# Seven block products of a float32 SwiGLU feed-forward: combining them on a seeded PSUM bank, and a third weight sum made by an adding transfer

## The chip, the cores and the metric

One core of one Trainium2 chip runs the whole program. The metric is device time in microseconds of one launch: the median of the runs of the kernel before is 1592.42 us (three runs, 1591.45 to 1592.46).

## The reference, cut to what matters

The reference is a small transformer of float32 arithmetic on 256 tokens of width 1024: two layers of (SwiGLU, mixer, SwiGLU), then two layers of (another mixer, SwiGLU). That makes six SwiGLU stages, called f = 0 to 5 below. Each is

```
gate, up = split(rms_norm(x) @ w_in)        # w_in 1024 x 5632, so 2816 columns each
x = x + factor * (silu(gate) * up) @ w_out  # w_out 2816 x 1024
```

Only these six stages are touched by the change.

## The kernel before, in words

**Numbers and engines.** Every float32 product is made from two rounded parts of each operand. A unit of weights is 128 x 2048 numbers (1 MB). It lands in `raw` (3 slots) or in one of the areas `up_k0`, `up_k1`, `w_sum`, `t2` of `work`; ScalarE writes its rounded part into `whi` (`hi`, L1098), VectorE writes the rest, source minus `whi`, into `wlo` (`lo`, L1614), and TensorE makes three matmuls for each pair of chunks (L2254 to L2256 in `product`). `whi` and `wlo` have 3 slots, used in turn: the rounding of unit u waits until TensorE is done with unit u - 3 (`unit_done`). Each engine works its own list strictly in the order in which the functions below write it out.

**A stage.** 42 units in a fixed order. The gate and up columns are cut into 11 blocks of 256: five "plain" blocks (PLAIN_UNITS, two units of 24 matmuls each) and three groups of two blocks, each group made by the seven products of a fast matrix scheme (SUM_UNITS, seven units of 12 matmuls each, `summed`). The four blocks of the product are gate and up for the two halves of tokens t = 0 and 1. The seven products want combinations of weights (`first_sum`, `second_sum`, `third_sum`, and a fourth that GpSimd's queue makes by an adding transfer, `added_block`) and combinations of the operand (`joined_operand`, `form`, with their two rounded parts `form_hi_part` and `form_lo_part`). Then come 11 down units of 24 matmuls (`down`), each behind the transposes of its activation (`turn`) and their two rounded parts (`product_hi` on ScalarE, `product_lo` on VectorE).

**Start of a stage.** Units 0 to 2 are rounded by the stage before. When the reciprocal norm is ready (GpSimd, L801), ScalarE rounds unit 3 and then makes `silu(0, 0)` and `silu(0, 1)` between its parts of the forms; VectorE makes `joined_operand` (L1700), four forms (L1708), the rest of unit 3, the rest of form 0 (L1712), then `product(0, 0)` and `product(0, 1)` (L1685). TensorE meanwhile makes `plain(1, 0, 0)` and `plain(1, 1, 0)`, then turns the first activation (`turn(b_y, act, 0, 2)`, L2375), which waits for both products; then `plain(1, 0, 1)` and `plain(1, 1, 1)`, which want unit 3, then `summed(0, 0)` (unit 4), then `plain(2, 0, 0)`, which waits for `act_ready` 4, that is for `product(1, 0)` and `product(1, 1)`. In stage 0 `begin_first` rounds unit 3 too.

**A group i.** VectorE: `first_sum` (L1629), `second_sum` (L1636), `third_sum` (L1639), six combinations of 128 x 512 from PSUM (`combine_z`, `_u`, `_w`, `_up1`, `_up0`, `_gate1`, L1654 to L1674) and the products. ScalarE: `first_product` copies the first product out of PSUM (L1144). SyncE issues the loads; the load into `up_k0` for a later group waits for the third sum. In group 0 the down unit 10 (`down(0)`) follows units 8 and 9.

**GpSimd** issues the fourth sum's transfers (L826) in order with the norms, `spread_table` and `attention_bias`, where a step waits for a unit of TensorE.

Of the kernel before, what the change touches and what calls it, by code (L numbers as in the profile page):

```python
# [23 lines left out]
ALU = mybir.AluOpType  # L24
# [52 lines left out]
COMBINED = 6  # L77
Z_AT, U_AT, W_AT, UP1_AT, UP0_AT, GATE1_AT = 1, 2, 3, 4, 5, 6
SUMS = 3
T1_AT, T2_AT, T3_AT = 1, 2, 3  # L80
# [96 lines left out]
class Signals:  # L177


    def __init__(self, sem):  # L180
# [19 lines left out]
        self.gate_bias_landed = sem("gate_bias_landed")  # L200
# [37 lines left out]
        self.p1_sb = sem("p1_sb")  # L238
# [111 lines left out]
def build(nc, a, out):  # L350

    with ExitStack() as ctx:
# [64 lines left out]
        pair_act, q_act = area(12288, TT, BANK), xn[:, 1, 0:BANK].rearrange("p (t c) -> p t c", t=TT)  # L417
        p1 = sb("p1", [P, BANK])
        zw, up1 = xn[:, 0, 0:BANK], xn[:, 0, BANK:D]
# [142 lines left out]
        def _(sp):  # L562
# [31 lines left out]
            def ffn(w_in, w_out, l, rnd, f, beside={}):  # L594
# [65 lines left out]
                for i in range(GROUPS):  # L660
                    if i:
                        sp.wait_ge(s.w_sum_ready, SUMS * (GROUPS * f + i - 1) + T3_AT)
                    up_block(i, 0, up_k0)
                    gate_block(i, 0)
                    if i:
                        sp.wait_ge(s.w_lo_ready, unit(0, rnd) + SUM_UNITS[i - 1][5] + 4)
                    up_block(i, 1, up_k1)
                    plain(2 + i, 0)
                    plain(2 + i, 1)
                    gate_block(i, 1)  # L670
# [6 lines left out]
            for l in range(DEPTH):  # L677
# [19 lines left out]
                def gate_bias(t, half):  # L697
                    at = half * D
                    broadcast(gate[:, t, at:at + D], "mix_gate_bias", l * 2 * D + at, D, s.gate_bias_landed)
# [87 lines left out]
        def _(pool):  # L787
# [32 lines left out]
            def added_block(name, l, rnd, i):  # L820

                pool.wait_ge(s.w_lo_ready, unit(0, rnd) + SUM_UNITS[i][3] + 4)
                for k in range(2):
                    src = bass.AP(tensor=a[name].tensor, offset=l * (D * 2 * F) + (4 + 2 * k) * P * 2 * F + (2 + 3 * i) * FB,
                                  ap=[[2 * F, P], [2 * F * P, 2], [1, BANK]])
                    pool.dma_start(t2[:, 2 * k * BANK:2 * (k + 1) * BANK].rearrange("p (k n) -> p k n", k=2), src, accum_op=ALU.add)\  # L826
                        .then_inc(s.w_added, LOADED)

            def attention_bias(l, rnd):
# [15 lines left out]
            for l in range(DEPTH):  # L845
                (r1, _, _, _), (r2, _, _, _) = ffn_stages_a(l)
                norm(3 * l)
                if l == 0:
                    spread_table(0, r1)
                added_block("ffn1_w_in", l, r1, 0)  # L850
                attention_bias(l, r1 + 4)
                pool.wait_ge(s.consts_a_landed, 16)
                pool.wait_ge(s.bias_landed, 2 * BANDS * GRID_H * LOADED * (l + 1))
                for j in range(BANDS):
                    if j == 1:
                        added_block("ffn1_w_in", l, r1, 2)
# [29 lines left out]
                if l + 1 < DEPTH:  # L886
                    spread_table(l + 1, r2)
                for i in range(GROUPS):
                    added_block("ffn2_w_in", l, r2, i)
# [8 lines left out]
            for l in range(DEPTH):  # L898
# [86 lines left out]
                for i in range(GROUPS):  # L985
                    added_block("w_gate_up_2", l, ffn_stage_b(l)[0], i)
# [14 lines left out]
        def _(act_e):  # L1001
# [87 lines left out]
            def ffn(rnd, f, n, o):  # L1089
# [15 lines left out]
                def summed_hi(i, m):  # L1105
                    source, at = {1: (w_sum, T1_AT), 3: (t2, T2_AT), 4: (w_sum, T3_AT), 6: (t2, 0)}[m]
                    if at:
                        act_e.wait_ge(s.w_sum_ready, SUMS * (GROUPS * f + i) + at)
                    else:
# [21 lines left out]
                def pair_silu(i, t):  # L1131

                    if t == 0:
                        act_e.wait_ge(s.unit_done, unit(0, rnd) + SUM_UNITS[i][2] + 4)
# [1765 lines left out]
```

## Time and profile before

| | |
|---|---|
| median of the runs | 1592.42 us |
| profiled execution | 1590.86 us, span 1589.1 us |
| TensorE matmuls busy | 1566.1 us (99%) |
| VectorE busy | 1274.1 us (80%) |
| ScalarE busy | 902.6 us (57%) |
| GpSimd busy | 210.2 us (13%) |
| DMA | 327.29 MB, 206 GB/s mean |
| TensorE clock granted | 0.998 of full speed |

An engine is busy while one of its instructions runs. A matmul's entry lasts longer than the step from one matmul to the next, because they overlap, so the steps between starts are what counts for TensorE. The profiled execution is 1.6 us shorter than the median.

### The profile page before, as it was taken

Reading aid. Unit: us, or ns where it says so; the run is one execution under the profiler, and the core shown is the slowest. Engines: PE = TensorE matmul, PEld = TensorE weight load, DVE = VectorE, ACT = ScalarE, POOL = GpSimd, SP = SyncE. Lnnn points to the kernel's source line nnn. Section 1 sums busy time; section 2 is a strip of 40 time slices with the busy share of each in tenths; the row PEclk is TensorE's granted clock in tenths of the full one; section 3 lists DMA queues with packets and bytes.
Section 4 is the critical chain, followed back from the end, with each engine's and each line's share of the span. In section 5 each row is a group of like instructions: output and inputs, shape, how many; then the busy total and the mean of one; then the engine's idle time right before and its main releaser. Section 6 shows DMA issues by size and latency. Waiting matters only on the chain.

```text
span 1589.1 us, 18786 instructions
## 1 busy us (share of the span) xinstructions
PE 1566.1 (99%) x7346; PEld 1295.9 (82%) x7346; DVE 1274.1 (80%) x1181; ACT 902.6 (57%) x1000; POOL 210.2 (13%) x271
## 2 busy tenths in 40 slices
PE   8999999999999999999999999999999999999998
PEld 6788888887888878888888788888878888887886
DVE  7888856679887988875677888778888876898886
ACT  6555545645555545555565555566655556665554
POOL 1132112011000013211201000131100002110000
PEclk9999999999999999999999999999999999999999
DMA  9887665567766778766556776561877565277672
GB/s 309 260 235 215 232 209 165 185 212 214 246 194 176 240 231 242 215 225 211 156 177 212 248 236 211 163 218 54 265 221 231 197 191 170 99 253 228 191 211 92
DMA packets 182415, 327.29 MB, mean 206 GB/s; under 512 B 13028, under 2 KB 77944, under 8 KB 182328
## 3 DMA queue, kind: packets, MB, share of 16 engines
q1 hardware_dynamic: 169064, 300.66, 56.8%
q0 software_dynamic: 12960, 24.94, 8.7%
q8 instruction: 58, 0.95, 0.3%
q10 hardware_dynamic: 304, 0.50, 0.1%
q14 instruction: 29, 0.24, 0.0%
HBM read 322.88 MB, written 2.88 MB: 205 GB/s over the span
## 4 chain that ended last, share of the span: by engine, by line
PE 90%; DVE 6%; ACT 2%; issue 1%; POOL 1%; POOLq 0%; DVEq 0%; ACTq 0%
PE pg L2254 18%; PE pg L2256 18%; PE pg L2255 18%; PE acc L2254 10%; PE acc L2256 10%; PE acc L2255 10%; DVE wlo L1614 2%; PE pg L2375 2%; PE pg L2267 1%; DVE xn L1708 1%; DVE xn L1700 1%; DVE work L1639 1%; ACT whi L1098 1%; POOL ms L799 1%; ACT work L1015 0%
## 5 line engine op out<-in xcount | busy, mean ns | idle before, releaser
L2254 PE MATMUL pg<-whi,xTh 128*128 128x512 f32 (+1 forms) x1096 | 436.8, 399 | 0.1
L2256 PE MATMUL pg<-whi,xTl 128*128 128x512 f32 (+1 forms) x1096 | 426.7, 389 | 0.0
L2255 PE MATMUL pg<-wlo,xTh 128*128 128x512 f32 (+1 forms) x1096 | 426.2, 389 | 0.0
L1614 DVE TENSOR_TENSOR wlo<-raw,whi 128x2048 fp32r<-128x2048 f32 x143 | 328.8, 2299 | 51.0 <-ACT whi L1098 48.7
L1098 ACT ACTIVATE whi<-raw 128x2048 fp32r<-128x2048 f32 x143 | 274.1, 1917 | 150.1 <-PE pg L2256 81.9
L1512 DVE TENSOR_TENSOR wlo<-raw,whi 128x2048 fp32r<-128x2048 f32 (+1 forms) x87 | 198.6, 2283 | 59.4 <-ACT whi L1008 59.1
L2254 PEld LDWEIGHTS pg<-whi,xTh 128*128 128x128 f32 x1096 | 206.4, 188 | 43.7 <-DVE xTl L1527 1.4
L2256 PEld LDWEIGHTS pg<-whi,xTl 128*128 128x128 f32 x1096 | 206.1, 188 | 42.8
L1614 DVE TENSOR_TENSOR wlo<-work,whi 128x2048 fp32r<-128x2048 f32 x90 | 208.3, 2314 | 39.1 <-ACT whi L1098 39.1
L2255 PEld LDWEIGHTS pg<-wlo,xTh 128*128 128x128 f32 x1096 | 206.5, 188 | 40.3 <-issue 1.0
L2254 PE MATMUL acc<-whi,bTh 128*128 128x512 f32 (+1 forms) x572 | 227.7, 398 | 8.0 <-DVE wlo L1614 8.0
L1098 ACT ACTIVATE whi<-work 128x2048 fp32r<-128x2048 f32 x90 | 172.5, 1916 | 100.1 <-PE acc L2256 75.0
L2256 PE MATMUL acc<-whi,bTl 128*128 128x512 f32 (+1 forms) x572 | 222.8, 390 | 0.0
L2255 PE MATMUL acc<-wlo,bTh 128*128 128x512 f32 (+1 forms) x572 | 222.3, 389 | 0.0
L1008 ACT ACTIVATE whi<-raw 128x2048 fp32r<-128x2048 f32 (+1 forms) x87 | 165.1, 1899 | 61.6 <-PE acc L2256 37.0
L2254 PEld LDWEIGHTS acc<-whi,bTh 128*128 128x128 f32 x572 | 107.5, 188 | 31.5 <-issue 10.5
L2256 PEld LDWEIGHTS acc<-whi,bTl 128*128 128x128 f32 x572 | 107.4, 188 | 23.0
L2255 PEld LDWEIGHTS acc<-wlo,bTh 128*128 128x128 f32 x572 | 107.6, 188 | 20.5
L1154 ACT ACTIVATE bTh<-pg 128x512 fp32r<-128x512 f32 x66 | 39.6, 599 | 76.9 <-PE pg L2375 76.5
L2254 PE MATMUL pg<-whi,bTh 128*128 128x512 f32 (+1 forms) x178 | 69.3, 390 | 0.0
L2256 PE MATMUL pg<-whi,bTl 128*128 128x512 f32 (+1 forms) x178 | 69.1, 388 | 0.0
L2255 PE MATMUL pg<-wlo,bTh 128*128 128x512 f32 (+1 forms) x178 | 69.0, 388 | 0.0
(276 smaller groups left out, 1955.0 us busy)
## 6 DMA issues: line engine op xcount, KB each, us to landing
raw<-in_ffn_w_in SPq DMA_DIRECT2D x124, 512.0 KB, 5.5
raw<-in_ffn_w_out SPq DMA_DIRECT2D x88, 512.0 KB, 4.6
raw<-in_mix_w_in SPq DMA_DIRECT2D x64, 512.0 KB, 4.6
raw<-in_w_gate_up SPq DMA_DIRECT2D x64, 512.0 KB, 5.5
work<-in_ffn_w_in SPq DMA_DIRECT2D x48, 512.0 KB, 5.7
raw<-in_w_down SPq DMA_DIRECT2D x44, 512.0 KB, 4.4
work<-in_ffn_w_in POOLq DMA_DIRECT2D x24, 512.0 KB, 9.5
raw<-in_w_in SPq DMA_DIRECT2D x24, 512.0 KB, 5.3
```

The lines of the kernel that those rows point to most:

```text
L799: pool.tensor_tensor(sums, mean, eps[:, 0:n], ALU.add).then_inc(ms_sem, 1)
L1008: act_e.activation(whi[:, slot, 0:cols], raw[:, slot, 0:cols], ACT.Copy).then_inc(s.w_hi_ready, 1)
L1098: act_e.activation(whi[:, u % SLOTS, :], source, ACT.Copy).then_inc(s.w_hi_ready, 1)
L1154: act_e.activation(bTh[:, part, :], bank[:, :].rearrange("p (c n) -> p c n", c=2), ACT.Copy).then_inc(s.actT_hi, 1)
L1512: v.tensor_tensor(wlo[:, slot, 0:cols], raw[:, slot, 0:cols], f32(whi[:, slot, 0:cols]), ALU.subtract)\
L1614: v.tensor_tensor(wlo[:, u % SLOTS, :], source, f32(whi[:, u % SLOTS, :]), ALU.subtract).then_inc(s.w_lo_ready, 1)
L1639: v.tensor_tensor(w_sum, up_k0, up_k1, ALU.add).then_inc(s.w_sum_ready, 1)
L1700: v.tensor_tensor(xn[:, :, :].rearrange("p t d -> p (t d)"), f32(xTh[:, :, :]).rearrange("p k n -> p (k n)"), f32(xTl[:, :, :]).rearrange( ...
L2254: pe.matmul(dst, xh, wh, start=first and i == 0, stop=False, skip_group_check=onto)
L2255: pe.matmul(dst, xh, wl, start=False, stop=False, skip_group_check=onto)
L2256: mm = pe.matmul(dst, xl, wh, start=False, stop=last and i == len(pairs) - 1, skip_group_check=onto)
L2375: tr = pe.transpose(bank[:, c * T + t * P:c * T + (t + 1) * P], source[:, t, at + c * P:at + (c + 1) * P], ident[:, :])
```

## The change

- The order of the first six products of a group changes: product 2 is accumulated before product 1, and the order of the 42 units with it (SUM_UNITS, DOWN_UNITS).
- ScalarE copies the first product from bank `pg[0][0]` into bank `pg[0][1]` (`seed`); products 3, 4 and 6 are then accumulated on that bank by TensorE, and product 5 on top of product 1 in the other. Two further copies by ScalarE (`second_product`, `hold`) and two subtractions by VectorE (`combine_up1`, `combine_up0`) take the place of one copy and six combinations.
- VectorE's third sum goes; GpSimd's queue adds the second up block into `up_k0` by two adding transfers after the first sum.
- The activation of a group alternates between two areas; the first two turned activations go to `acc[2]` and `acc[3]`.
- The lists at the start of a stage are reordered on ScalarE and VectorE.

```diff
-SUM_UNITS = ((4, 6, 8, 9, 11, 13, 15), (16, 18, 20, 21, 23, 25, 27), (28, 30, 32, 33, 35, 37, 38))
+SUM_UNITS = ((4, 8, 6, 9, 11, 13, 15), (16, 20, 18, 21, 22, 24, 26), (28, 32, 30, 33, 34, 36, 38))
-DOWN_UNITS = (10, 12, 14, 22, 24, 26, 34, 36, 39, 40, 41)
+DOWN_UNITS = (10, 12, 14, 23, 25, 27, 35, 37, 39, 40, 41)
...
# SyncE, group i
-                        sp.wait_ge(s.w_sum_ready, SUMS * (GROUPS * f + i - 1) + T3_AT)
-                    up_block(i, 0, up_k0)
-                    gate_block(i, 0)
-                    if i:
+                        gate_block(i, 0)
+                        sp.wait_ge(s.w_lo_ready, unit(0, rnd) + SUM_UNITS[i - 1][4] + 4)
+                        up_block(i, 0, up_k0)
                         sp.wait_ge(s.w_lo_ready, unit(0, rnd) + SUM_UNITS[i - 1][5] + 4)
+                    else:
+                        if rnd == 0:
+                            sp.wait_ge(raw_landed[0], 64)
+                        up_block(i, 0, up_k0)
+                        gate_block(i, 0)
...
# GpSimd
+            def third_sum(name, l, f, i):
+
+                pool.wait_ge(s.w_sum_ready, SUMS * (GROUPS * f + i) + T1_AT)
+                added_block(name, l, i, 0, up_k0, s.w_third)
...
+                        if (j, row) == (1, 0):
+                            third_sum("ffn1_w_in", l, 2 * l, 1)
                         if (j, row) == (2, 1):
-                            added_block("ffn1_w_in", l, rnd - 4, 1)
+                            fourth_sum("ffn1_w_in", l, rnd - 4, 1)
...
# ScalarE
+                def seed(i):
+
+                    act_e.wait_ge(s.unit_done, unit(0, rnd) + SUM_UNITS[i][0] + 4)
...
+                    act_e.activation(pg[0][1][:, :], pg[0][0][:, :], ACT.Copy).then_inc(s.p_copied, 1)
+
+                def second_product(i):
...
+                    act_e.activation(up1, pg[0][0][:, :], ACT.Copy).then_inc(s.p_copied, 1)
+
+                def hold(i):
+                    act_e.wait_ge(s.unit_done, unit(0, rnd) + SUM_UNITS[i][3] + 4)
+                    act_e.activation(held[:, :], pg[0][1][:, :], ACT.Copy).then_inc(s.p_copied, 1)
...
-                if f > 0:
+                if f == 0:
+                    silu(0, 0)
+                    silu(0, 1)
+                    form_hi_part(0)
+                    form_hi_part(1)
+                    form_hi_part(2)
+                else:
+                    form_hi_part(0)
+                    silu(0, 0)
+                    form_hi_part(1)
+                    form_hi_part(2)
                     loaded_hi(3)
-                form_hi_part(0)
-                silu(0, 0)
-                silu(0, 1)
-                form_hi_part(1)
-                form_hi_part(2)
+                    silu(0, 1)
                 form_hi_part(3)
...
+                        summed_hi(i, 4)
+                        second_product(i)
+                        silu(2 + i, 1)
+                        loaded_hi(DOWN_UNITS[3 * i])
+                        hold(i)
...
# VectorE
+                if start:
+                    product(0, 0)
+                    product(0, 1)
                 joined_operand()
                 form(0)
                 form(1)
+                form_lo_part(0)
+                if not start:
+                    product(0, 0)
                 form(2)
+                form_lo_part(1)
+                form_lo_part(2)
                 form(3)
                 if not start:
                     loaded_lo(3)
-                form_lo_part(0)
-                product(0, 0)
-                product(0, 1)
-                form_lo_part(1)
+                    product(0, 1)
                 first_sum(0)
                 for i in range(GROUPS):
                     qa, qb = PLAIN_UNITS[2 + i]
                     loaded_lo(SUM_UNITS[i][0])
+                    second_sum(i)
                     if i == 0:
                         product_lo(0)
+                    else:
+                        pair_product(i - 1, 0)
                     loaded_lo(qa)
                     if i == 0:
                         product(1, 0)
                         product(1, 1)
...
# TensorE, group i
+                    copied(i, SEED_AT)
+                    summed(i, 2, b_x, x_block(0, 1), onto=True)
                     plain(2 + i, 0, 1).then_inc(s.ffn_t0_done, 1)
                     plain(2 + i, 1, 1).then_inc(s.unit_done, 1)
-                    pe.wait_ge(s.p1_sb, GROUPS * f + i + 1)
-                    summed(i, 2, b_x, x_block(0, 1), onto=True)
+                    pe.wait_ge(s.silu_ready, ACTS * f + 4 + 4 * i + 1)
...
+                    summed(i, 1, b_x, x_form(0))
...
+                    summed(i, 3, b_y, x_form(2), onto=True)
                     if i:
                         turn_first(i - 1, True)
...
+                    else:
+                        down(0)
+                    copied(i, HELD_AT)
...
+                    summed(i, 4, b_y, x_form(1), onto=True)
+                    if i:
+                        down(3 * i, lambda: turn_first(i - 1, False))
```

## Rows read from the trace of the kernel before

**Rows 1.** The page: engines, and the chain that ended last.

```profile
PE 1566.1 (99%) x7346; PEld 1295.9 (82%) x7346; DVE 1274.1 (80%) x1181; ACT 902.6 (57%) x1000; POOL 210.2 (13%) x271
...
PE 90%; DVE 6%; ACT 2%; issue 1%; POOL 1%; POOLq 0%; DVEq 0%; ACTq 0%
```

**Rows 2.** Waits of TensorE: us in total, times, longest us.

```profile
PE acc L2254 <- DVE wlo L1614: 8.0, 6, 1.3
PE pg L2375 <- DVE work L1685: 6.5, 6, 3.5
```

**Rows 3.** Timeline of the start of stage 3: start us, us, instruction, idle before it.

```profile
866.26 0.55 POOL L801 TENSOR_TENSOR rstd<-ms,neghalf 128x1 f32<-128x1 f32 x1
...
866.85 1.92 ACT L1098 ACTIVATE whi<-raw 128x2048 fp32r<-128x2048 f32 x1 [2.60 <-POOL rstd L801]
866.85 2.29 DVE L1700 TENSOR_TENSOR xn<-xTh,xTl 128x2048 f32<-128x2048 f32 x1 [0.71 <-POOL rstd L801]
...
869.18 2.62 DVE L1708 TENSOR_TENSOR xn<-xn 128x512 f32<-128x512 f32 x4
...
869.90 0.63 ACT L1148 ACTIVATE bTh<-xn 128x512 fp32r<-128x512 f32 x1 [1.13 <-DVE xn L1708]
...
870.55 1.28 ACT L1129 ACT_TABLE_LOAD   x1
...
871.85 0.84 ACT L1129 ACTIVATE work<-pg,rstd 128x256 f32<-128x256 f32 x2
...
871.96 0.39 PE L2254 MATMUL pg<-whi,xTh 128*128 128x512 f32 x1
...
874.46 0.39 PE L2256 MATMUL pg<-whi,xTl 128*128 128x512 f32 x1
874.52 0.87 DVE L1685 SCALAR_TENSOR_TENSOR work<-pg,rstd,work 128x256 f32<-128x256 f32 x2
...
875.44 0.66 PE L2375 MATMUL pg<-ident,work 128*128 128x128 f32 x4 [0.60 <-DVE work L1685]
```

**Rows 4.** The same timeline, up to the second pair of products.

```profile
878.11 2.28 DVE L1614 TENSOR_TENSOR wlo<-raw,whi 128x2048 fp32r<-128x2048 f32 x1
...
880.31 0.68 DVE L1692 TENSOR_TENSOR bTl<-pg,bTh 128x512 fp32r<-128x512 f32 x1
...
880.91 2.28 DVE L1614 TENSOR_TENSOR wlo<-raw,whi 128x2048 fp32r<-128x2048 f32 x1
...
883.11 0.87 DVE L1685 SCALAR_TENSOR_TENSOR work<-pg,rstd,work 128x256 f32<-128x256 f32 x2
...
884.03 0.19 PEld L2254 LDWEIGHTS pg<-whi,xTh 128*128 128x128 f32 x1 [0.17 <-DVE work L1685]
```

**Rows 5.** Timeline of stage 2: its first two silu follow the form directly.

```profile
538.67 0.82 ACT L1129 ACTIVATE work<-pg,rstd 128x256 f32<-128x256 f32 x2
```

**Rows 6.** Timeline of the start of stage 0.

```profile
22.54 2.28 DVE L1700 TENSOR_TENSOR xn<-xTh,xTl 128x2048 f32<-128x2048 f32 x1
...
28.92 1.12 PE L2375 MATMUL pg<-ident,work 128*128 128x128 f32 x4 [3.52 <-DVE work L1685]
...
39.13 0.60 ACT L1144 ACTIVATE p<-pg 128x512 f32<-128x512 f32 x1 [0.43 <-PE pg L2256]
```

**Rows 7.** Groups of instructions by line and form: busy us, mean ns, idle before.

```profile
L1098 ACT ACTIVATE whi<-work 128x2048 fp32r<-128x2048 f32 x90 | 172.5, 1916 | 100.1 <-PE acc L2256 75.0 <-PE pg L2256 14.5 <-DVE work L1639 10.7
...
L1639 DVE TENSOR_TENSOR work<-work 128x2048 f32<-128x2048 f32 x18 | 41.1, 2283 | 0.0
...
L1662 DVE TENSOR_TENSOR xn<-xn,pg 128x512 f32<-128x512 f32 x18 | 12.2, 679 | 0.0
...
L1144 ACT ACTIVATE p<-pg 128x512 f32<-128x512 f32 x18 | 10.8, 601 | 3.0 <-PE pg L2256 2.6
```

**Rows 8.** The adding transfers of line 826, and the DMA queues' shares.

```profile
L826 POOL DMA_DIRECT2D work<-in_ffn_w_in x24: 1204/1487/1790, 55.4 to 997.7; - x24
...
DMA to landing us min/median/max: 5.7/9.4/12.1
```

**Rows 9.** The page: DMA queues, packets, MB, share of 16 engines.

```profile
q1 hardware_dynamic: 169064, 300.66, 56.8%
q0 software_dynamic: 12960, 24.94, 8.7%
```

More of the change, by code:

```diff
@@ L1619, in summed_lo @@
                 def summed_lo(i, m):
[L1620 removed]
+                    lo(SUM_UNITS[i][m], {1: w_sum, 3: t2, 4: up_k0, 5: up_k1, 6: t2}[m])
                 def sums_before(i):
@@ L1759, in ffn @@
-                    loaded_lo(DOWN_UNITS[3 * i])
-                    if i:
+                        loaded_lo(DOWN_UNITS[0])
+                        product(2, 1)
+                        summed_lo(0, 4)
+                        loaded_lo(DOWN_UNITS[1])
+                        summed_lo(0, 5)
+                        combine_up1(0)
+                        loaded_lo(DOWN_UNITS[2])
+                        product_lo(2)
+                        first_sum(1)
+                        summed_lo(0, 6)
@@ L1761, in ffn @@
+                        combine_up0(0)
+                    else:
+                        summed_lo(i, 4)
+                        product(2 + i, 1)
+                        loaded_lo(DOWN_UNITS[3 * i])
                         product_lo(3 * i)
-                    product(2 + i, 1)
-                    combine_u(i)
-                    summed_lo(i, 4)
-                    if i:
+                        summed_lo(i, 5)
+                        combine_up1(i)
+                        loaded_lo(DOWN_UNITS[3 * i + 1])
@@ L2378, in turn_first @@
                 def turn_first(i, first):
-                    turn(pg[1][1 - first], pair_act, 0 if first else FB, ACTS if i == GROUPS - 1 else 4 + 4 * (i + 1) + (1 if first else 2))
+                    turn(pg[1][1 - first], pair_acts[i % 2], 0 if first else FB, ACTS if i == GROUPS - 1 else 4 + 4 * (i + 1) + (1 if first else 2))
                 def turn_plain(i):
@@ L2401, in combined, with copied @@
                     pe.wait_ge(s.combined, COMBINED * (GROUPS * f + i) + at)
+                def copied(i, at):
+                    pe.wait_ge(s.p_copied, COPIES * (GROUPS * f + i) + at)
                 def form_ready(m):
@@ L2450, in ffn @@
                 plain(1, 1, 0).then_inc(s.unit_done, 1)
-                turn(b_y, act, 0, 2)
+                turn(acc[2], act, 0, 2)
                 plain(1, 0, 1).then_inc(s.ffn_t0_done, 1)
@@ L2482, in ffn @@
                     if i == 0:
                         form_ready(1)
-                    summed(i, 4, b_y, x_form(1))
-                    down(3 * i + 1, lambda: turn_plain(i))
-                    pe.wait_ge(s.silu_ready, ACTS * f + 4 + 4 * i + 3)
+                    summed(i, 4, b_y, x_form(1), onto=True)
+                    if i:
+                        down(3 * i, lambda: turn_first(i - 1, False))
+                    else:
+                        down(1, lambda: turn_plain(0))
                     if i == 0:
@@ L2488, in ffn @@
                         form_ready(3)
-                    summed(i, 5, b_x, x_form(3))
-                    if i < GROUPS - 1:
-                        down(3 * i + 2)
+                    summed(i, 5, b_x, x_form(3), onto=True)
+                    if i:
+                        down(3 * i + 1, lambda: turn_plain(i))
+                    else:
+                        down(2)
                     combined(i, UP1_AT)
                     summed(i, 6, b_y, x_block(1, 1), onto=True)
-                down(8, lambda: turn_first(GROUPS - 1, True))
+                    if i:
+                        down(3 * i + 2, (lambda: turn_first(i, True)) if i == GROUPS - 1 else None)
```

235 lines of the change are left out of this document (97 added, 138 removed).

## The prediction

> **What bounds the kernel now.** I read the page first, then TensorE's waits, then the timeline where those waits stand. TensorE has a matmul running for 1566.1 of 1589.1 us and makes 90% of the chain that ended last [rows 1]: nothing shortens the kernel unless TensorE idles less, because the change leaves the number of matmuls and transposes as it is. Its waits in the six stages are two kinds [rows 2]: `down(0)` waits for the rest of unit 10, 8.0 us in six waits, because VectorE makes the third sum ahead of it; and the first turn waits for `product(0, 1)`, 6.5 us in six waits, of which stage 0 alone has 3.5 and the others 0.6 each. So some 14.5 us, under 1%, is all that the change can win. VectorE's busy 80% matters only through what TensorE waits for.
>
> **Scales.** TensorE: 11 steps from 871.96 to 874.46 us [rows 3], 0.227 us a matmul, so a summed unit takes 2.72 us and a plain or down unit 5.44. VectorE: a 128x2048 subtraction or sum gives way to the next instruction after 2.20 us and a 128x512 one after 0.60 [rows 4]; if the next needs its result, 2.28 and 0.69. ScalarE: 1.92 for a unit [rows 7], 0.63 for a form, 0.60 for a 128x512 copy.
>
> **Taken off.** VectorE loses 18 third sums of 2.28 us and 18 times four combinations of 0.68, about 90 us [rows 7]. With it `down(0)` no longer waits: counted from the products that open a stage's group 0, unit 10's rest would be done after some 18.5 us, and TensorE wants it at 19.5. Gain 8.0 us, and this is all that TensorE gains from it, since elsewhere it does not wait.
>
> **Stages 1 to 5, up to the first turn.** This is the largest term. ScalarE rounded unit 3 at once (866.85 us) while VectorE joined the operand; now it comes behind form 2, and `product(0, 1)` comes behind unit 3's rest. I follow stage 3 by the rows of before [rows 3]. The join starts at 866.85, form 0 is done at 869.87, ScalarE rounds it by 870.53, the table load (1.28) ends at 871.83, `silu(0, 0)` (0.48) at 872.33. VectorE, standing in order, makes `product(0, 0)` from 872.36 and form 2 from 872.76 to 873.45. ScalarE rounds form 2 until 874.11 and, overlapping by 0.1, unit 3 from 874.00 to 875.92. VectorE has filled the time with two form rests and form 3, and waits: unit 3's rest 875.95 to 878.24, `product(0, 1)` from 878.15 to 878.62. TensorE starts the turn at 878.67 in place of 875.44. It was there at 874.7, so its wait grows from 0.6 to about 4.0 us.
>
> **From there to `plain(2, 0, 0)`.** VectorE's list from 878.55: first sum 2.20, unit 4 2.20, second sum 2.20 (moved ahead), rest of the turned activation 0.60, unit 5 2.20, two products 0.87, end at 888.82. Before, the products ended at 883.98 [rows 4]. TensorE's own work from the turn to that point took until 884.03, less the 0.17 of waiting [rows 3, 4], so 8.4 us: it would be ready at 887.1, up to 1 us later if matmuls are slow after the longer wait, as in stage 0, whose turn took 1.12 us [rows 6] and not 0.66. VectorE is later, so it sets this point: 4.84 us later than before in stages 1, 3, 4 and 5. Stage 2 has no table load [rows 5], so everything behind the silu is 1.2 us earlier: 3.6. The sum is 4 x 4.84 + 3.6 = 23.0 us. After that VectorE gains on TensorE, as the margins at units 6 (3 us), 7 (3.4) and 8 (3.7) show when its list is laid out, so nothing more is lost and nothing is won back.
>
> The Trainium skill (ScalarE: Activation LUTs, What ACT_TABLE_LOAD costs) states 1283 ns for the load and another 1380 ns of draining for each switch of set. The row has the load at 1.28 us and the silu 0.02 us behind it, so no such drain stands there; by the rule the silu would come 1.38 us later in each of four stages, and the total would be 5.5 us more.
>
> **Stage 0.** The two products move ahead of the join, whose start slips from 22.54 [rows 6] to 23.3. The turn then needs 23.4 and TensorE arrives at 25.25: the 3.5 us go. But VectorE's list (join, four forms, three rests, first sum, unit 4) ends at 35.1, where TensorE wants unit 4 at 31.2; with second sum, activation, unit 5 and two products it reaches 40.9. Before, this point was 38.9 (the copy at 39.13 less 0.2 of latency) [rows 6]. Cost 2.0. The bounds are 0 (the list is as late as before) and 5 (the load of `up_k0`, now held behind unit 3's, lands later).
>
> **The new wait of groups 1 and 2.** Product 4 goes on the bank that `hold` must have copied; between them TensorE has only a turn. Clock zero where unit 19 is done: TensorE finishes 20 at 2.72, 21 at 5.44, and the turn takes about 0.4 (its entry of 0.66 [rows 3] less the overlap with the next matmul, an estimate), so it arrives at 5.8. ScalarE: unit 20's copy from 2.92, a silu, then unit 23 (1.92, overlapped) from 3.86 to 5.78, then `hold` 5.70 to 6.30 by the 0.60 of the copy of before [rows 7]. Wait 0.5 us, twelve times: 6.0 us. A lower bound is zero, if the turn covers it; the upper is 0.9, if ScalarE is late by another small step. In group 0 `down(0)` stands between and covers 5.44 us.
>
> **At nothing.** `seed` (0.6) has a plain unit of 5.44 us beside it; `second_product` is waited for a unit later. Group 0's two copies lie beside the down units. SyncE's loads of `up_k0` wait for a rest that is done some 20 us before the next first sum. The third sum's transfer: two issues on GpSimd at 1.49 us and 9.4 until landed (12.1 at most) [rows 8], so 12 to 15 us after the first sum. Its reader, product 4's unit, is rounded over 20 us after it in group 0. In the first SwiGLU of a layer GpSimd's queue delays group 1's to unit 15 done plus two bias issues; unit 22 can be rounded 16.3 us after unit 15, plus a summed unit: a margin of 3 to 5 us. The bytes are 18.9 MB more, about 6.6% of the DMA engines' time at that queue's present price [rows 9] (8.7% for 24.94 MB), beside 65% in use: room enough.
>
> **Sum.** 23.0 + 2.0 + 6.0 - 8.0 = +23.0 us on the profiled execution's 1590.9, so 1613.9. The median stands 1.6 above that execution: 1615 us.
>
> **Rivals.**
> - *The start costs less* (1596 to 1606): if VectorE or ScalarE finish their lists some 1.5 us sooner in every stage than I laid out, and `hold` is covered, the terms are 5 x 2.5 + 2 - 8, or about +6 to +10. The table load row speaks against it. Chance 0.11.
> - *Faster* (1580): the start's dependencies don't reach the turn, so that the turn's wait stays at 0.6, stage 0's 3.5 goes and `hold` is covered: 1592.4 - 8.0 - 4.5 = 1580. The place is `product(0, 1)` in stages 1 to 5, and the point is 8 us: TensorE arrives 7.9 us after both other engines start, and the chain I count is 11.8 us. It has to be 3.8 us shorter. For it speaks that VectorE has 90 us less to do and that TensorE may hide lateness of weights inside matmul durations. Against it: the matmuls step at 0.227 us nearly everywhere. Chance 0.13.
> - *No change* (1590 to 1595): the start costs about 10 us and is paid by the waits removed. Chance 0.04.
> - *The third sum lands late* (1630 to 1650): the adding transfer is 12 us or slower beside more traffic, the rounding of unit 22 or 34 waits on ScalarE with everything queued behind it, some 2 us in 12 groups on top of the sum. The margin of 3 us decides. Chance 0.06.
> - That the change doesn't do what it says can be left out: the third sum's instruction is gone from VectorE's list.
>
> **How the numbers follow.** The forecast (1606 to 1624) has 0.66. With the lesser cost and a little of the late transfer the range 1597 to 1630 holds 0.8. A difference under 0.2% (3.2 us) can't be told from none here. Faster: 0.13. Same: 0.04. Slower: 0.66 + 0.11 + 0.06 = 0.83.
>
> **What would show it.** In TensorE's waits the line of `down(0)` is gone; the line of the turn has five waits near 4 us (3 in stage 2) and none in stage 0; a new line of matmuls behind the second pair of products; and twelve short waits for ScalarE's copy of the bank. In the timeline unit 3 is rounded behind form 2. If the turn's waits are under 1 us the forecast falls at its main step; if ScalarE waits for the adding transfer, the fourth rival holds.

## The result and the profile after

The changed kernel takes 1622.86 us (median of 4 runs, 1620.67 to 1626.88) against 1591.93 us of the kernel before on the same chip (4 runs, 1589.67 to 1592.46): a ratio of 1.020, 95% interval 1.0176 to 1.0224, so 31 us slower. Forecast were 1615 us and slower, with a range of 1597 to 1630. The profiled execution of the changed kernel took 1624.3 us, with a span of 1622.4.

The page of the changed kernel: busy time of each engine, the two large DMA queues, and the engines on the chain that ended last.

```profile
PE 1580.2 (97%) x7346; PEld 1303.5 (80%) x7346; DVE 1194.0 (74%) x1091; ACT 919.9 (57%) x1036; POOL 249.9 (15%) x307
...
q1 hardware_dynamic: 169064, 300.66, 55.1%
q0 software_dynamic: 22752, 43.82, 15.4%
...
PE 80%; DVE 6%; DMA 5%; ACT 4%; issue 2%; POOL 1%; SPq 0%; POOLq 0%; DVEq 0%; ACTq 0%
```

VectorE has 80 us less to do than before [rows 1] and the kernel is 31 us slower. TensorE runs as many matmuls; its busy time grew by 14 us. Its share of the chain fell from 90% to 80%, and VectorE, ScalarE and DMA transfers took it. GpSimd's queue took 8.7% of the DMA engines' time before [rows 9] and takes 15.4% now.

What TensorE waits for in the changed kernel (engine, tile and line of the waiting instruction, what released it, total us, times, longest us):

```profile
PE acc L2391 <- DVE work L1703: 18.3, 5, 3.9
PE pg L2270 <- DVE wlo L1660: 9.4, 8, 3.8
PE pg L2270 <- ACT held L1178: 2.7, 11, 0.3
PE pg L2270 <- DVE work L1703: 2.5, 2, 1.3
```

The first line is the first turn (`turn_first`), 6.5 us in six waits before [rows 2]; the line of `down(0)` of before, 8.0 us, is gone; the third is the wait for `hold`, and the fourth one for products, in two places. The second, 9.4 us for rests of weight units, is in the forecast only in part (3.78 us of it is unit 4 in stage 0), and what stands behind the rest shows in the same view for ScalarE:

```profile
ACT whi L1118 <- DMA raw<-in_ffn_w_in: 44.4, 16, 7.0
```

The timeline of stage 3, on ScalarE and VectorE from the join to the turn (start, duration, engine, line, operation, out<-in, and in brackets the idle time before it and its releaser):

```profile
883.47 2.29 DVE L1718 TENSOR_TENSOR xn<-xTh,xTl 128x2048 f32<-128x2048 f32 x1 [0.71 <-POOL rstd L807]
...
887.23 1.28 ACT L1151 ACT_TABLE_LOAD   x1
...
888.53 0.47 ACT L1151 ACTIVATE work<-pg,rstd 128x256 f32<-128x256 f32 x1
...
890.69 1.89 ACT L1118 ACTIVATE whi<-raw 128x2048 fp32r<-128x2048 f32 x1
...
892.62 2.29 DVE L1660 TENSOR_TENSOR wlo<-raw,whi 128x2048 fp32r<-128x2048 f32 x1 [0.51 <-ACT whi L1118]
894.83 0.48 DVE L1703 SCALAR_TENSOR_TENSOR work<-pg,rstd,work 128x256 f32<-128x256 f32 x1
...
895.36 0.98 PE L2391 MATMUL acc<-ident,work 128*128 128x128 f32 x4 [3.90 <-DVE work L1703]
```

The join of this stage starts at 883.47, that is 16.62 us later than before [rows 3]. With that offset taken off, unit 3's rest starts at 876.00 (forecast 875.95), `product(0, 1)` at 878.21 (878.15), and the turn at 878.74 (878.67) after a wait of 3.90 us (4.0).

The same stage, ten microseconds on (SPq is SyncE's queue):

```profile
897.80 2.46 POOL L830 DMA_DIRECT2D work<-in_ffn_w_in  x2 [14.37 <-DVE work L1675]
899.73 1.58 SPq L604 DMA_DIRECT2D raw<-in_ffn_w_in  x2
...
910.38 1.92 ACT L1118 ACTIVATE whi<-raw 128x2048 fp32r<-128x2048 f32 x1 [3.94 <-DMA raw<-in_ffn_w_in]
```

The first row is the third sum's two adding transfers, right behind the first sum. The second is the load of unit 7, and ScalarE gets it 10.65 us after the issue. In the kernel before it is the seventh unit loaded and its buffer comes free with unit 3's rest; now unit 6 is loaded ahead of it, so it is the eighth and waits for unit 4's rest.

### The profile page after: what moved, and what is told of

Read it like the earlier page. It is cut to its first block, busy times and chain, and to the rows that moved or that the text cites. A ratio compares the mean times of both kernels' runs of the same rounds, so it can differ in the third digit from the quotient of the medians.

```text
span 1622.4 us, 18719 instructions
## 1 busy us (share of the span) xinstructions
PE 1580.2 (97%) x7346; PEld 1303.5 (80%) x7346; DVE 1194.0 (74%) x1091; ACT 919.9 (57%) x1036; POOL 249.9 (15%) x307
## 3 DMA queue, kind: packets, MB, share of 16 engines
q1 hardware_dynamic: 169064, 300.66, 55.1%
q0 software_dynamic: 22752, 43.82, 15.4%
## 4 chain that ended last, share of the span: by engine, by line
PE 80%; DVE 6%; DMA 5%; ACT 4%; issue 2%; POOL 1%; SPq 0%; POOLq 0%; DVEq 0%; ACTq 0%
PE pg L2270 16%; PE pg L2272 16%; PE pg L2271 16%; PE acc L2270 9%; PE acc L2272 9%; PE acc L2271 9%; DMA raw<-in_ffn_w_in 4%; DVE wlo L1660 2%; ACT whi L1118 2%; PE pg L2283 1%; PE pg L2391 1%; DVE xn L1718 1%; DMA raw<-in_w_gate_up 1%; POOL ms L805 1%; DVE work L1675 1%
## 5 line engine op out<-in xcount | busy, mean ns | idle before, releaser
L2270 PE MATMUL pg<-whi,xTh 128*128 128x512 f32 (+1 forms) x1096 | 441.9, 403 | 11.5 <-DVE wlo L1660 9.0
L2272 PE MATMUL pg<-whi,xTl 128*128 128x512 f32 (+1 forms) x1096 | 430.2, 392 | 0.0
L2270 PEld LDWEIGHTS pg<-whi,xTh 128*128 128x128 f32 x1096 | 208.7, 190 | 59.7 <-DVE wlo L1660 12.5
L2272 PEld LDWEIGHTS pg<-whi,xTl 128*128 128x128 f32 x1096 | 208.4, 190 | 43.6
L2270 PE MATMUL acc<-whi,bTh 128*128 128x512 f32 (+1 forms) x572 | 227.2, 397 | 0.1
L2272 PE MATMUL acc<-whi,bTl 128*128 128x512 f32 (+1 forms) x572 | 223.0, 390 | 0.0
L2272 PEld LDWEIGHTS acc<-whi,bTl 128*128 128x128 f32 x572 | 107.4, 188 | 22.9
L2270 PEld LDWEIGHTS acc<-whi,bTh 128*128 128x128 f32 x572 | 107.5, 188 | 21.1 <-DVE bTl L1710 0.5
L830 POOL DMA_DIRECT2D work<-in_ffn_w_in x48 | 59.3, 1476 | 262.6 <-DVE work L1675 139.4
L2270 PE MATMUL pg<-whi,bTh 128*128 128x512 f32 (+1 forms) x178 | 70.8, 398 | 3.2 <-ACT held L1178 2.7
L805 POOL TENSOR_TENSOR ms<-ss,eps 128x1 f32<-128x1 f32 x16 | 19.2, 1198 | 350.3 <-ACT work L1035 350.3
```

Of the source, the lines that this page charges most:

```text
L805: pool.tensor_tensor(sums, mean, eps[:, 0:n], ALU.add).then_inc(ms_sem, 1)
L830: pool.dma_start(dst[:, 2 * k * BANK:2 * (k + 1) * BANK].rearrange("p (k n) -> p k n", k=2), src, accum_op=ALU.add)\
L2270: pe.matmul(dst, xh, wh, start=first and i == 0, stop=False, skip_group_check=onto)
L2272: mm = pe.matmul(dst, xl, wh, start=False, stop=last and i == len(pairs) - 1, skip_group_check=onto)
```

## The experiments

Two theories stood against each other. *The start*: the order of the two lists at a stage's start makes the turn and `plain(2, 0, 0)` late, as forecast, and the loss falls with it. *The transfers*: the 36 adding transfers delay loads, and the loss falls with them. All kernels ran beside the kernel before, whose median stayed between 1590.99 and 1591.5 us.

### e1_start_order: another order at the start

Of the changed kernel; ScalarE rounds unit 3 while VectorE joins, as before, and both silus come right behind form 0. VectorE's calls move from between the forms, where their lines go, to behind unit 3's rest:

```diff
@@ ScalarE, f > 0
+                    loaded_hi(3)
                     form_hi_part(0)
                     silu(0, 0)
+                    silu(0, 1)
                     form_hi_part(1)
                     form_hi_part(2)
-                    loaded_hi(3)
-                    silu(0, 1)
@@ VectorE, f > 0
                     loaded_lo(3)
+                    form_lo_part(0)
+                    product(0, 0)
                     product(0, 1)
+                    form_lo_part(1)
+                    form_lo_part(2)
                 first_sum(0)
```

> The changed kernel with the lists of ScalarE and VectorE at the start of stages 1 to 5 in the order of the kernel before (unit 3 rounded first, both products behind form 0); the second sum stays where the change put it. Queue-order theory: the five waits at the first turn (18.3 us in the changed kernel) fall to about 0.6 each, but VectorE's list up to plain(2, 0, 0) is only 2.0 us shorter (0.8 in stage 2), because the moved second sum and form 2's rest are still in it, so a new wait of 2 to 3 us appears there and the total falls by only some 9 us, to about 1614. Transfer theory (the extra adding transfers are the main cost): the turn's waits go but the total falls by less than 5 us. If the turn's waits alone were the loss: 16 us or more less, under 1607.

Measured: 1614.64 us, ratio 1.0146 (1.0129 to 1.0163), so 8 us off, as expected. TensorE's waits:

```profile
PE pg L2274 <- DVE work L1703: 13.0, 6, 2.5
...
PE acc L2395 <- DVE work L1703: 3.0, 5, 0.6
```

The turn is back at 0.6 us a stage, as before [rows 2], so the order on record made that wait. VectorE is still late, with 2.5 us at `plain(2, 0, 0)`, since the second sum stands ahead of it.

### e2_second_sum and e3_both: the second sum behind the second pair of products

e2 is the changed kernel with this edit, e3 has e1's too:

```diff
                     loaded_lo(SUM_UNITS[i][0])
-                    second_sum(i)
+                    if i:
+                        second_sum(i)
                     if i == 0:
@@
                         product(1, 1)
+                        second_sum(0)
                         form_lo_part(3)
```

> The changed kernel with only the second sum of group 0 moved back behind the second pair of products. Queue-order theory: the waits at the turn stay at 3.9 us, TensorE is behind anyway, and only the waits of 1.2 to 1.3 us at plain(2, 0, 0) in stages 0 and 2 go: some 3 us less, about 1620. If the second sum were a loss by itself, 5 x 2.2 = 11 us less.

> Both edits together. Queue-order theory: VectorE's list is 4.2 us shorter in each of stages 1 to 5 than in the changed kernel, so about 20 us less, near 1603: more than the sum of the two alone (9 and 3). Transfer theory: 1612 or more.

Measured: e2 1627.6 us (1.023, 1.0215 to 1.0245), e3 1623.82 us (1.0207, 1.0192 to 1.0222). Both are misses, and e3 is the larger: almost no lateness of the start is left in it (the turn's waits are 3.0 us in five), and yet it takes as long as the changed kernel. TensorE's waits in e3:

```profile
PE pg L2276 <- DVE wlo L1660: 24.8, 10, 5.5
```

and the timeline of its stage 1:

```profile
373.73 2.50 POOL L830 DMA_DIRECT2D work<-in_ffn_w_in  x2 [12.44 <-DVE work L1675]
375.50 1.51 SPq L604 DMA_DIRECT2D raw<-in_ffn_w_in  x2
...
389.21 1.91 ACT L1118 ACTIVATE whi<-raw 128x2048 fp32r<-128x2048 f32 x1 [9.83 <-DMA raw<-in_ffn_w_in]
...
393.50 0.80 PE L2276 MATMUL pg<-whi,xTh 128*128 128x512 f32 x1 [5.47 <-DVE wlo L1660]
```

Unit 7's load is issued 1.8 us behind the adding transfers, at 375.50, and ScalarE has it at 389.21, after 13.7 us; TensorE waits 5.47 us at unit 7. What e1 gains at the turn, e3 loses a little further on.

That e2 is slower than the changed kernel is not shown: its runs (1625.12 to 1629.79) overlap with those of the changed kernel (1620.67 to 1626.88), and the spans of the two profiled executions, 1623.2 and 1622.4, differ by 0.8 us. That it isn't 3 us faster its stage 3 explains:

```profile
883.98 2.29 DVE L1718 TENSOR_TENSOR xn<-xTh,xTl 128x2048 f32<-128x2048 f32 x1 [0.71 <-POOL rstd L807]
...
904.14 0.48 DVE L1703 SCALAR_TENSOR_TENSOR work<-pg,rstd,work 128x256 f32<-128x256 f32 x1 [0.73 <-ACT work L1151]
...
906.15 0.39 PE L2272 MATMUL pg<-whi,xTh 128*128 128x512 f32 x1
```

The products of the second pair are done at 904.62, and TensorE comes to `plain(2, 0, 0)` at 906.15, without a wait and 22.17 us behind the join. In the changed kernel that matmul stands at 905.65, 22.18 us behind its join at 883.47. VectorE is early now, and TensorE comes no earlier. In stage 2, where the changed kernel waited 1.34 us for the products, e2 has slow matmuls in place of the wait (shown in the last section).

### e4_third_on_vector and e5_both_vector: the third sum made by VectorE again

e4 is the changed kernel without the 36 adding transfers of `third_sum`, e5 is e3 without them; the sum is made in place:

```diff
             def third_sum(name, l, f, i):
+                return
...
+                def own_third_sum(i):
+                    v.tensor_tensor(up_k0, up_k0, up_k1, ALU.add).then_inc(s.w_third, 2 * LOADED)
...
                     summed_lo(i, 1)
+                    if i:
+                        own_third_sum(i)
                     summed_lo(i, 3)
@@ group 0
                         loaded_lo(DOWN_UNITS[0])
+                        own_third_sum(0)
                         product(2, 1)
```

> The changed kernel with the third sum made by VectorE (in place, up_k0 + up_k1, behind unit 10's rest in group 0 and behind product 2's unit in the others), and the 36 adding transfers of it left out. Transfer theory: ScalarE's waits for raw<-in_ffn_w_in (44.4 us in 16 waits) shrink to some 10 us, the waits of TensorE for wlo (9.4 us in 8) fall by half or more, and the total by 5 to 10 us. Queue-order theory alone: the total stays within 3 us of the changed kernel, because the turn's waits stay and VectorE has room for the sum.

> e3_both with the third sum made by VectorE and its adding transfers left out. New theory after e3_both: with the lists repaired TensorE is earlier, and the next late thing is unit 7's load (issued behind unit 4's rest, 13.7 us to land in stage 1), late because the two adding transfers of the third sum are issued just ahead of it into DMA engines that are 90% busy there. Then TensorE's waits for wlo (24.8 us in 10) fall to some 5 (stage 0's 3.7 stays), and the total to about 1597. Rival (unit 7's load is late because the new order of the units makes it wait for unit 4's rest in place of unit 3's): the waits stay above 15 us and the total above 1610.

Measured: e4 1623.47 us (1.0202, 1.0186 to 1.0217), the time of the changed kernel; e5 1600.03 us (1.005, 1.0033 to 1.0067). The same edit is worth nothing in the one and 24 us in the other. In e4 that is a balance: TensorE waits for unit 7 in no stage, which the changed kernel pays with some 8 us, but VectorE's own sum costs about as much elsewhere. TensorE waits for `hold` 17 times in place of 11 and once 2.1 us for a weight rest, some 5 us together, and behind the turn of stage 5 there are more slow matmuls, 1.3 us. In e3 the waits for unit 7 are far longer, so more is gained. ScalarE's waits for loads of this weight, in e4 and in e5:

```profile
ACT whi L1118 <- DMA raw<-in_ffn_w_in: 17.0, 9, 5.1
...
ACT whi L1118 <- DMA raw<-in_ffn_w_in: 21.2, 11, 5.0
```

Against 44.4 us in the changed kernel and 53.7 in e3: the transfers were what delayed the loads. The order of the units is the new one in e4 and e5 too, so unit 7's later buffer alone costs TensorE nothing there.

### e6_both_deferred: the same bytes, later

e3 again, with the adding transfers of group 0 held until ScalarE has rounded unit 7, so that its load has landed. This tells the amount of traffic from its place:

```diff
                 pool.wait_ge(s.w_sum_ready, SUMS * (GROUPS * f + i) + T1_AT)
+                if i == 0:
+                    pool.wait_ge(s.w_hi_ready, unit(0, FFN_STARTS[f]) + PLAIN_UNITS[2][1] + 1)
                 added_block(name, l, i, 0, up_k0, s.w_third)
```

> e3_both with the adding transfers kept, but those of group 0 held on GpSimd until unit 7's rounded part is made. Theory of the transfers' place: the same bytes at another time, so unit 7 lands in time as in e5_both_vector and the total is about 1598. Rival (adding transfers cost by their amount wherever they are): waits for other units take the place of unit 7's, total above 1610. Rival of the list order: unchanged at 1624.

Measured: 1595.64 us (1.0028, 1.0016 to 1.004; 6 runs), 28 us less than e3 with every byte still moved. Its stage 1, against that of e3 above:

```profile
368.15 0.92 SPq L604 DMA_DIRECT2D raw<-in_ffn_w_in  x2
...
373.59 1.92 ACT L1120 ACTIVATE whi<-raw 128x2048 fp32r<-128x2048 f32 x1 [1.53 <-DMA raw<-in_ffn_w_in]
...
376.22 2.50 POOL L830 DMA_DIRECT2D work<-in_ffn_w_in  x2 [22.28 <-ACT whi L1120]
```

The same load lands in 5.4 us, not 13.7. So it is the place of the transfers and not their amount. e6 is also 4 us faster than e5, which has none of these transfers but VectorE's sum in their stead.

### e7_before_third_late and e9_before_third_early: what `down(0)` costs in the kernel before

Nothing of the change is in these two; only group 0's third sum has another place in VectorE's list. It costs TensorE 8.0 us where it stands [rows 2]. e7, then e9:

```diff
                         summed_lo(i, 3)
-                        third_sum(i)
                         product(2 + i, 0)
@@
                         product_lo(3 * i)
+                    else:
+                        third_sum(0)
```

```diff
                     if i == 0:
-                        summed_lo(i, 3)
                         third_sum(i)
+                        summed_lo(i, 3)
                         product(2 + i, 0)
```

> The kernel before with VectorE's third sum of group 0 moved behind the rest of unit 10, nothing else. If the third sum's place alone made down(0) wait, its 8.0 us go and the ratio is 0.995 (1583); ScalarE's rounding of unit 11 comes 2.3 us later and has down(0)'s 5.4 us to hide in. Rival: the wait moves to unit 11 and the ratio is 1.000.

> The kernel before with VectorE's third sum of group 0 ahead of the rest of unit 9, in the 2.81 us in which VectorE waits there for ScalarE, and nothing else. e7_before_third_late won 4 us and left 4.0 us in six waits for combine_w. If the idle gap takes the sum whole, neither wait is left: 8 us less than the kernel before, ratio 0.995. Rival (the sum pushes unit 9's rest and the wait comes back at unit 9): ratio 0.998 or more.

Measured: e7 1587.37 us (0.9976, 0.9967 to 0.9986; 9 runs), half of what was expected, since the later place brings a new wait at the combination behind it:

```profile
PE pg L2255 <- DVE xn L1662: 4.0, 6, 0.7
```

e9 1581.77 us (0.9939, 0.9927 to 0.9952), 10 us off. VectorE stood idle for 2.81 us behind the first combination of group 0 in stage 3 of the kernel before, waiting for ScalarE. The kernel before:

```profile
898.00 2.29 DVE L1614 TENSOR_TENSOR wlo<-work,whi 128x2048 fp32r<-128x2048 f32 x1 [2.81 <-ACT whi L1098]
```

There the sum now goes (e9):

```profile
891.15 2.28 DVE L1639 TENSOR_TENSOR work<-work 128x2048 f32<-128x2048 f32 x1
894.09 2.29 DVE L1614 TENSOR_TENSOR wlo<-work,whi 128x2048 fp32r<-128x2048 f32 x1 [0.65 <-ACT whi L1098]
```

The idle 2.81 us have become 0.65, and the waits at `down(0)` are gone.

### e8_deferred_hold: `hold` ahead of the down unit

e6, with `hold` moved ahead of the rounding of the down unit, to take away TensorE's short wait for it:

```diff
                         silu(2 + i, 1)
-                        loaded_hi(DOWN_UNITS[3 * i])
                         hold(i)
+                        loaded_hi(DOWN_UNITS[3 * i])
                         product_hi(3 * i)
```

> e6_both_deferred with hold ahead of the rounding of the next down unit on ScalarE in groups 1 and 2. The waits of TensorE for that copy (2.8 us in 11) go to zero: 3 us less than e6_both_deferred. If the wait is the copy's own latency behind product 3, at most 1 us less.

Measured: 1619.77 us (1.0176, 1.0161 to 1.0191), 24 us more than e6 where 3 less were expected. ScalarE now waits at `hold` 21.5 us in twelve waits, and TensorE for the activation's rest:

```profile
PE acc L2278 <- DVE bTl L1712: 20.5, 12, 1.7
```

ScalarE stands in front of `hold` until TensorE is done with the bank, and the rounding behind it comes late by as much, twelve times.

TensorE's wait for `hold` stays as it was, 2.8 us in eleven, so the second of the two cases expected holds: it is the copy's own time and not the rounding ahead of it. The same place in stage 0 of the changed kernel and of e8, the turn, the copy and the matmul that wants it:

```profile
111.31 0.60 PE L2391 MATMUL pg<-ident,work 128*128 128x128 f32 x4
111.50 0.60 ACT L1178 ACTIVATE held<-pg 128x512 f32<-128x512 f32 x1
...
112.15 0.50 PE L2270 MATMUL pg<-whi,bTh 128*128 128x512 f32 x1 [0.25 <-ACT held L1178]
```

```profile
107.35 0.60 PE L2399 MATMUL pg<-ident,work 128*128 128x128 f32 x4
107.55 0.60 ACT L1180 ACTIVATE held<-pg 128x512 f32<-128x512 f32 x1 [1.85 <-PE pg L2280]
...
108.20 0.50 PE L2278 MATMUL pg<-whi,bTh 128*128 128x512 f32 x1 [0.25 <-ACT held L1180]
```

In both, the matmul starts 0.84 to 0.85 us behind the turn. Behind the 111 turns of the changed kernel with no wait it is 0.35 in the median, so each wait costs 0.5 us and the twelve 6.0.

### e10_before_third_start and e11_deferred_start: the start once more

e10 is e9 (the kernel before, third sum moved) and e11 is e6 (the change), both with the products right behind unit 3's rest, and `form_lo_part` 1 to 3 later, behind unit 7's rest in e10 and behind unit 6's in e11. e10's edit:

```diff
@@ ScalarE (stage 0: both silus ahead of form 0)
-                form_hi_part(0)
+                    form_hi_part(0)
                 silu(0, 0)
                 silu(0, 1)
+                if f == 0:
+                    form_hi_part(0)
@@ VectorE
+                if start:
+                    product(0, 0)
+                    product(0, 1)
                 joined_operand()
...
                 form(1)
-                form(2)
-                form(3)
                 if not start:
                     loaded_lo(3)
+                    product(0, 0)
+                    product(0, 1)
+                form(2)
+                form(3)
                 form_lo_part(0)
-                product(0, 0)
-                product(0, 1)
-                form_lo_part(1)
                 first_sum(0)
...
                     if i == 0:
+                        form_lo_part(1)
                         form_lo_part(2)
```

> e9_before_third_early, and at the start of a stage only what the turn needs ahead of it: both products directly behind unit 3's rest (in stage 0 ahead of the joined operand), the rests of forms 1 to 3 behind unit 7's. The turn's waits (0.6 in five stages, 3.5 in stage 0) go; VectorE's list up to plain(2, 0, 0) is 0.6 us shorter, in stage 0 about 3: some 6 us less than e9_before_third_early, ratio 0.991. Rival (VectorE's list, not its order, sets plain(2, 0, 0)): 2 us less or nothing.

> e6_both_deferred with the same start (products behind unit 3's rest, rests of forms 1 to 3 behind unit 6's). The five waits of 0.6 at the turn and of 0.3 at plain(2, 0, 0) go: 5 us less than e6_both_deferred, about 1591, so the change's combining and its adding transfers together come out level with the kernel before. If it were 8 us less, the relief of VectorE would be worth something by itself.

Measured: e10 1577.44 us (0.9911, 0.9896 to 0.9927), the fastest kernel of the study, faster than both kernels and 4.3 us below e9, where 6 were expected; e11 1589.99 us (0.9989, 0.998 to 0.9998; 10 runs). e10's page and TensorE's longest wait in the six stages:

```profile
PE 1564.7 (99%) x7346; PEld 1296.1 (82%) x7346; DVE 1274.2 (81%) x1181; ACT 903.6 (57%) x1000; POOL 210.5 (13%) x271
```

```profile
PE pg L2259 <- DVE wlo L1616: 2.0, 1, 2.0
```

VectorE has its full 1274 us of work and TensorE is 99% busy. The same start on the change (e11) brings it 1.5 us below the kernel before, less than the 3.2 us that can be told from none, and leaves it 12.5 us behind e10.

## Why the prediction was right, and where it was not

**Taken off: right.** The waits of `down(0)` are gone, and that is worth 9.4 us, not 8.0 (see the sum). VectorE's busy time fell by 80 us and not 90, since its entries overlap: by the steps of 2.20 and 0.60 us the 18 sums and 72 combinations make 83. That this is all that the relief of VectorE is worth was also right: e9 gets the same wait away with all of VectorE's work in place, and gains 10 us.

**Up to the first turn: right.** It waits 18.3 us in five waits, 3.9 in four stages and 2.7 in stage 2 (forecast 4.0 and 3.0). e1 takes the order back and the turn is at 0.6 us again.

**Up to `plain(2, 0, 0)`: right in size, the reason only half.** In stage 3 its first weight load stands at 905.54, which is 888.92 on the clock of before, against a forecast of 888.82:

```profile
905.54 0.19 PEld L2270 LDWEIGHTS pg<-whi,xTh 128*128 128x128 f32 x1 [0.16 <-DVE work L1703]
...
905.65 0.40 PE L2270 MATMUL pg<-whi,xTh 128*128 128x512 f32 x1
```

The wait there is only 0.16 us, and the "up to 1 us later if matmuls are slow" was really 1.6 (10.02 us from the turn to here less the wait, against 8.4), so that TensorE and VectorE arrive together. The forecast said that VectorE sets this point. That holds in stages 0 and 2, where TensorE waits 1.17 and 1.34 us. In stages 1, 3, 4 and 5 TensorE's slow matmuls alone make it as late: e2 takes 2.2 us out of VectorE's list and the point stays. That two paths came out level there was luck.

**The table load: no drain here.** The Trainium skill (ScalarE: Activation LUTs, What ACT_TABLE_LOAD costs) adds 1380 ns of draining to the load. This trace doesn't agree: after the change too the silu starts at 888.53, 0.02 us behind the load's end at 888.51, and the places of the steps follow without a drain.

**Stage 0: the sign was right, the end was not followed far enough.** The turn's wait of 3.5 us is gone. TensorE waits for unit 4 (35.10) and the products (40.89, forecast 40.9), and then once more:

```profile
35.10 0.57 PE L2270 MATMUL pg<-whi,xTh 128*128 128x512 f32 x1 [3.78 <-DVE wlo L1660]
40.89 0.49 PE L2270 MATMUL pg<-whi,xTh 128*128 128x512 f32 x1 [1.17 <-DVE work L1703]
51.65 0.50 PE L2270 MATMUL pg<-whi,xTh 128*128 128x512 f32 x1 [1.83 <-DVE wlo L1660]
```

The last is unit 7, late by its load. Unit 4's wait is what "ends at 35.1, where TensorE wants unit 4 at 31.2" said.

**The wait for `hold`: right size, wrong reason.** Forecast 0.5 us twelve times. The view lists 0.25 us eleven times, 2.7 in all, but it counts idle time from the end of an entry, and entries overlap; between starts it is the 0.5 us, twelve times (e8 above). The forecast had `hold` stand behind the rounding of unit 23. With that rounding behind it, in e8, the wait is the same: what TensorE waits for is the copy, which can't start before product 3 is done and is longer than the turn beside it. That both reckonings give 0.5 was luck.

**At nothing: the step that failed.** "The bytes are 18.9 MB more [...] beside 65% in use: room enough" looked at the amount only, and the margin was counted for the reader of the third sum and not for a load beside it. Unit 7's load comes one buffer later, behind unit 4's rest, and that is right behind the adding transfers. The new order of units was read in the diff for the products, and not for SyncE's list of loads. The fourth rival looked for a late adding transfer; the transfers were in time (8.0 us to landing in the median, under the 9.4 of [rows 8]; ScalarE waits for one of them once, 2.6 us) and made another load late. It is paid on the line of the weight rests: of its 9.4 us 3.78 are unit 4 in stage 0 and some 4.4 unit 7 in four stages; the other 1.2 are three short waits in later groups.

**The sum.** Forecast +23.0, measured +31 (+33.3 between the spans of the two profiled executions). Both traces hold all 7346 matmuls, so each matmul can be set against the one of the same number before, and how much later it starts shows what each stretch costs, waits and slow matmuls together:

| stretch | forecast, us | worked out, us |
|---|---|---|
| to `plain(2, 0, 0)`, stages 1 to 5 | +23.0 | +24.1 (5.9, 3.6, 4.9, 4.9, 4.8) |
| the same in stage 0 | +2.0 | +2.0 |
| from there to `down(0)`: unit 7 | 0 | +7.7, half of it in stage 0 |
| `down(0)` | -8.0 | -9.4 |
| rest of the six stages | +6.0 | +8.9 |
| sum | +23.0 | +33.3 |

Of the 8.9 us 6.0 are the waits for `hold`; the other 2.9 stand in stages 0, 2 and 3, where the three short waits are. So the miss of 10 us is unit 7's load for the greater part. The forecast's other terms came out within 1.5 us each, two of them (VectorE setting `plain(2, 0, 0)`, and the reason for `hold`) partly by luck. The measured 1622.9 is still inside the forecast of 1606 to 1624, but a third of the 33 us stands where the sum had nothing.

**How the two causes hide one another.** Taking the start off alone brings 8 us (e1), taking it off altogether none (e3), taking the transfers off alone none (e4, where VectorE's own sum eats the gain); both together bring 23 (e5) and 27 (e6). Once TensorE no longer waits at the turn, it arrives at unit 7 before the load does: by the same reckoning the stretch with unit 7 costs 7.7 us in the changed kernel and 29.5 in e3. Had only e3 and e4 been run, both theories would have looked refuted.

## What to carry to other kernels

A change of the order in which units are used also changes which buffer each load waits for: follow every load to its new release, and ask what else is issued in the microseconds around it. A mean DMA share says nothing about one load, and of two causes in series neither shows its size when it is taken away alone, so try them together. A wait for a copy is not always shortened by making the copy's engine free sooner; look first whether the copy could start sooner (e8 cost 24 us). And before work is taken off an engine that is not the bound, look for its idle gap: moving one sum into 2.8 us of idle time was worth 10 us here, while taking 80 us of work away was worth no more.

## What the runs showed of the hardware

**What a wait costs beyond itself.** After the 3.9 us wait of the turn in stage 3 TensorE's next matmuls (L2270 to L2272) stand 0.43 us apart and not 0.23 as in [rows 3]:

```profile
896.56 0.63 PE L2271 MATMUL pg<-wlo,xTh 128*128 128x512 f32 x1
896.99 0.63 PE L2272 MATMUL pg<-whi,xTl 128*128 128x512 f32 x1
```

The stretches behind the turn say the same by the clock (stretch, its length, busy time and count on TensorE, weight loads, VectorE, ScalarE and GpSimd, granted clock, DMA share, GB/s): the changed kernel in stages 1 and 3, then the kernel before in stage 3, where the wait was 0.6 us.

```profile
371.10:377.00 5.90, 5.81 (x16) 4.74 (x17) 5.90 (x4) 2.39 (x2) 3.21 (x4) 0.52 0.73 201
895.30:899.50 4.20, 4.14 (x13) 3.47 (x14) 4.20 (x3) 2.40 (x2) 1.70 (x2) 0.59 0.74 251
```

```profile
875.40:879.60 4.20, 4.16 (x21) 3.51 (x22) 4.20 (x3) 3.53 (x4) 0.00 (x0) 1.00 0.76 242
```

A granted clock of 0.52 is close to the lower level of 1.2 GHz; before it is the full 2.4. Thirteen instructions in 4.2 us in place of 21: by the matmuls of the same number, a wait of 3.9 us costs TensorE 1.5 to 1.6 us more in stages 3, 4 and 5 and 2.6 in stage 1, and it shows in the profile as busy time. It is no fixed price: the turn's wait in stage 2 is 2.71 us in the changed kernel and in e2, and behind it the clock is full in the first and near the lower level in the second, which there loses 1.6 us. The same stretch of both, the changed kernel first:

```profile
558.50:562.50 4.00, 3.92 (x19) 3.32 (x20) 4.00 (x3) 2.88 (x3) 1.48 (x2) 1.00 0.77 251
...
558.50:562.50 4.00, 4.00 (x13) 3.31 (x14) 4.00 (x2) 2.40 (x2) 1.57 (x2) 0.57 0.80 258
```

The mean granted clock of the whole execution follows: 0.998 before, 0.992 in the changed kernel, 0.989 in e2 and 0.998 again in e6.

**Adding transfers beside a load.** Two adding transfers of 512 KB, issued 1.8 us ahead, made the load of 1 MB take 13.7 us (e3) in place of 5.4 (e6). In stage 1 of e3 the DMA share of the stretch around them is 0.90:

```profile
369.50:393.50 24.00, 17.77 (x80) 14.14 (x81) 16.90 (x14) 11.05 (x11) 7.39 (x8) 0.99 0.90 251
```

The Trainium skill (DMA: Bandwidth & Descriptors, Queues, rings and completion order) states that each DMA engine serves the queues that it has work for in turn, a packet at a time. A second queue would then take turns from the first, and the two landings agree with this; how the turns were shared out was not measured. By the shares of the queues a byte of GpSimd's took more time than one of SyncE's: 15.4% for 43.82 MB against 55.1% for 300.66 MB, so 0.35 against 0.18% per MB.

**Left open.** What decides whether the clock falls behind a wait of 2.7 us; the 2.9 us in the rest of the stages, of which the three short waits explain only a part; and what unit 7's load in its old place in the order would bring, since that order was not undone by itself (with the new order and no adding transfer beside it, in e4, TensorE doesn't wait for it).
